# Delta rule gate stage in channel order: 512-column gate products, outputs turned on their own, gating in PSUM

## What is computed

```python
def gated_rmsnorm(o, w, gate):
    o = o * lax.rsqrt(jnp.mean(o * o, -1, keepdims=True) + RMS_EPS)
    return o * w.astype(jnp.float32) * jax.nn.silu(gate.astype(jnp.float32))

def gdn_mixer(x, w_in, conv_w, a_log, dt_bias, norm_w, w_out):
    p = x @ w_in
    qkv = causal_conv_silu(p[..., :GDN_QKV], conv_w)
    rest = p[..., GDN_QKV:]
    gate = rest[..., :GDN_VAL].reshape(B, T, GDN_HEADS, GDN_DV)
    ...
    o = gated_delta_rule(q, k, v, g, beta)
    o = gated_rmsnorm(o, norm_w, gate)
    return o.reshape(B, T, GDN_VAL).astype(x.dtype) @ w_out

x = layer_norm(DEEP_ALPHA * x + y, ln_g[i], ln_b[i])   # y: the mixer's result
```

## Time and profile before

| | |
|---|---|
| median of three runs | 1319.94 us (1319.39 to 1321.54) |
| the profiled execution | 1322.95 us |
| its span, first to last instruction | 1321.2 us |
| TensorE busy | 1232.3 us, 93% of the span |
| DVE, ScalarE, POOL busy | 600.3, 504.2, 382.8 us |
| granted TensorE clock, mean of the span | 0.967 |

### The profile page before, as it was taken

One profiled execution on the slowest core, in us unless ns is written; L12 is line 12 of the kernel. 1 busy time (PEld: TensorE's weight loads), 2 busy tenths in 40 slices (PEclk: granted clock), 3 DMA queues, 4 the chain that ended last, 5 costly groups with the idle time before them and its releaser, 6 DMA issues.

```text
span 1321.2 us, 17053 instructions
## 1 busy us (share of the span) xinstructions
PE 1232.3 (93%) x6956; PEld 1050.5 (80%) x6956; DVE 600.3 (45%) x869; ACT 504.2 (38%) x621; POOL 382.8 (29%) x92
## 2 busy tenths in 40 slices
PE   5879999999999979999999999888899799999986
PEld 5568878888788858888798878888788568999875
DVE  1473353343622255569724466444500614443614
ACT  4255434444211136643434235122221533335423
POOL 0014443444344423233212110222234225233111
PEclk9889999999999989999999999998999899999988
DMA  9983222222322332232312120111232322221101
GB/s 352 386 293 112 95 84 75 95 95 95 114 96 96 96 132 65 64 96 64 102 59 64 33 96 1 37 61 63 68 124 96 100 66 96 64 65 65 64 0 64
DMA packets 108349, 128.66 MB, mean 97 GB/s; under 512 B 13033, under 2 KB 98925, under 8 KB 108157
## 3 DMA queue, kind: packets, MB, share of 16 engines
q1 hardware_dynamic: 103412, 120.69, 27.5%
q10 hardware_dynamic: 4873, 7.04, 1.5%
HBM read 122.48 MB, written 5.24 MB: 97 GB/s over the span
## 4 chain that ended last, share of the span: by engine, by line
PE 41%; DVE 8%; ACT 2%; issue 1%; DVEq 0%; ACTq 0%
PE ps L243 10%; PE ps L244 9%; PE ps L245 9%; DVE val L1345 4%; PE ps L1480 3%; PE ps L2062 2%; PE ps L1823 1%; PE ps L1831 1%; PE ps L1860 1%; PE ps L1951 1%; PE ps L1957 1%; PE ps L1952 1%; DVE gate_silu L1341 1%; ACT gate_silu L735 1%; PE ps L2081 1%
## 5 line engine op out<-in xcount | busy, mean ns | idle before, releaser
L365 POOL TENSOR_TENSOR wl<-raw,wh 128x2048 fp32r<-128x2048 f32 x81 | 378.6, 4674 | 910.1 <-ACT wh L390 910.1
L390 ACT ACTIVATE wh<-raw 128x2048 fp32r<-128x2048 f32 x81 | 154.9, 1912 | 389.2 <-PE ps L245 389.2
L243 PE MATMUL ps<-xth,wh 128*128 128x512 f32 x672 | 270.2, 402 | 4.4 <-DVE xtl L960 3.7
L245 PE MATMUL ps<-xth,wl 128*128 128x512 f32 x672 | 263.7, 392 | 0.0
L244 PE MATMUL ps<-xtl,wh 128*128 128x512 f32 x672 | 263.5, 392 | 0.0
L243 PE MATMUL ps<-wh,xth 128*128 128x256 f32 (+1 forms) x576 | 176.0, 306 | 3.4 <-DVE xtl L853 3.4
L244 PE MATMUL ps<-wl,xth 128*128 128x256 f32 (+1 forms) x576 | 174.0, 302 | 0.0
L245 PE MATMUL ps<-wh,xtl 128*128 128x256 f32 (+1 forms) x576 | 173.4, 301 | 0.0
L243 PEld LDWEIGHTS ps<-xth,wh 128*128 128x128 f32 x672 | 127.4, 190 | 31.0 <-issue 6.5
L245 PEld LDWEIGHTS ps<-xth,wl 128*128 128x128 f32 x672 | 127.2, 189 | 27.6
L244 PEld LDWEIGHTS ps<-xtl,wh 128*128 128x128 f32 x672 | 127.5, 190 | 24.4
(11 more groups left out here) (287 smaller groups left out, 1766.7 us busy)
## 6 DMA issues: line engine op xcount, KB each, us to landing
ada<-in_ada_w SPq DMA_DIRECT2D x24, 1024.0 KB, 10.8
raw<-in_gdn_w_in SPq DMA_DIRECT2D x24, 1024.0 KB, 5.1
raw<-in_ffn_w_up SPq DMA_DIRECT2D x22, 1024.0 KB, 5.0
raw<-in_gla_w_in SPq DMA_DIRECT2D x12, 1024.0 KB, 5.0
raw<-in_ffn_w_down SPq DMA_DIRECT2D x11, 1024.0 KB, 4.8
raw<-in_gdn_w_out SPq DMA_DIRECT2D x8, 1024.0 KB, 4.8
raw<-in_gla_w_out SPq DMA_DIRECT2D x4, 1024.0 KB, 4.9
xres<-in_x SPq DMA_DIRECT2D x4, 512.0 KB, 5.8
```

The costliest lines, as they stand in the source:

```text
L243: nc.tensor.matmul(o, lh, rh, start=first, stop=False)
L245: return nc.tensor.matmul(o, ll, rh, start=False, stop=last)
L365: nc.gpsimd.tensor_tensor(wl[:, s, :], raw[:, s, :], wh[:, s, :].bitcast(f32), ALU.subtract)\
L390: nc.scalar.activation(wh[:, s, :], raw[:, s, :], ACT.Copy).then_inc(hi_done, 1)
```

## The change

- The gate is made with `col_chunk`: two pieces p = 2h and 2h + 1 of 128 channels per unit, 48 products of 512 columns, each piece in one of the banks 0 to 3.
- ScalarE scales the outputs of a head by `coef` in token order (`output_scale`, four operations), and TensorE turns them without the gate (`turn_outputs(h)`), in the middle of the second piece of the same head's unit.
- The gate times the norm weight times the turned outputs is one DVE operation per piece, in place in PSUM banks 4 to 7. The norm weight is a column there, one number per partition: it comes in with the rows at the start (`bgk_norm`, one more DMA in ScalarE's queue), and the row `norm_w` goes.
- Silu, high part and low part are made per piece; `ogt_h` and `ogt_l` are laid out by channel.
- In unit 0 of the output projection the token tiles come in the order 0, 2, 1, 3, with a wait ahead of each of the last three.

```diff
...
-    bgk_col = at("bgk_col", CONST + 5888, [LH])
+    bgk_norm = at("bgk_norm", CONST + 5888, [LH + DV // P])
...
-    gate_silu = at("gate_silu", PH + 96 * KB, [2, TT, DV])
+    gate_silu = at("gate_silu", PH + 96 * KB, [4, T])
...
-    ogt_h = at("ogt_h", PH + 32 * KB, [TT, 2 * H, P], f32r)
-    ogt_l = at("ogt_l", PH + 64 * KB, [TT, 2 * H, P], f32r)
+    ogt_h = at("ogt_h", PH + 32 * KB, [2 * H, T], f32r)
+    ogt_l = at("ogt_l", PH + 64 * KB, [2 * H, T], f32r)
...
+            act.dma_start(rows[12:14, 0, :], a["gdn_norm_w_2"][0].rearrange("(k n) -> k n", n=P)).then_inc(S("rows_in"), 16)
...
-            row(norm_w[:], a["gdn_norm_w_2"][0], "alog_in")
...
-            def gated_high(h):
-                act.wait_ge(S("og_turned"), h + 1)
-                nc.scalar.activation(ogt_h[:, :, 2 * h:2 * h + 2, :].rearrange("p t k n -> p k t n"),
-                                     bank2(4 + 2 * (h % 2)).rearrange("p (k t n) -> p k t n", k=2, n=P), ACT.Copy).then_inc(S("ogt_hi"), 1)
+            def output_scale(h):
+                act.wait_ge(S("coef_done"), 1)
+                for tt in range(TT):
+                    sc = nc.scalar.activation(val[:, tt, h, :], val[:, tt, h, :], ACT.Copy, scale=coef[:, 3, tt, h:h + 1])
+                sc.then_inc(S("o_scaled"), 1)
+            def gate_activation(p):
+                if p % 2 == 0:
+                    act.wait_ge(S("gate_half"), p // 2 + 1)
+                else:
+                    act.wait_ge(w_used, U_GIN + GIN_QK + GIN_V + p // 2 + 1)
+                if p >= 4:
+                    act.wait_ge(S("og_done"), p - 3)
+                nc.scalar.activation(gate_silu[:, p % 4, :], ps[:, p % 4, :], ACT.Silu).then_inc(S("gate_done"), 1)
+            def gated_high(p):
+                act.wait_ge(S("og_done"), p + 1)
+                nc.scalar.activation(ogt_h[:, p, :], ps[:, 4 + p % 4, :], ACT.Copy).then_inc(S("ogt_hi"), 1)
+            output_scale(0)
+            output_scale(1)
             for h in range(H):
-                act.wait_ge(w_used, U_GIN + GIN_QK + GIN_V + h + 1)
-                if h >= 2:
-                    act.wait_ge(S("og_done"), h - 1)
-                nc.scalar.activation(gate_silu[:, h % 2], bank2(2 * (h % 2)).rearrange("p (t n) -> p t n", n=DV), ACT.Silu)\
-                    .then_inc(S("gate_done"), 1)
+                gate_activation(2 * h)
+                gated_high(2 * h)
+                gate_activation(2 * h + 1)
+                gated_high(2 * h + 1)
                 high_gin(GIN_QK + GIN_V + h + 2)
-                if h >= 1:
-                    gated_high(h - 1)
-            gated_high(H - 1)
-            act.wait_ge(S("og_done"), H)
+                if h + 2 < H:
+                    output_scale(h + 2)
...
-            step(V.tensor_tensor(coef[:, 3], coef[:, 2], scal[:, QS], ALU.mult))
-            def gated_low(h):
-                v.wait_ge(S("ogt_hi"), h + 1)
-                dst = ogt_l[:, :, 2 * h:2 * h + 2, :].rearrange("p t k n -> p k t n")
-                hi = ogt_h[:, :, 2 * h:2 * h + 2, :].rearrange("p t k n -> p k t n")
-                V.tensor_tensor(dst, bank2(4 + 2 * (h % 2)).rearrange("p (k t n) -> p k t n", k=2, n=P), hi.bitcast(f32), ALU.subtract)\
-                    .then_inc(S("ogt_lo"), 1)
-            for h in range(H):
-                v.wait_ge(S("gate_done"), h + 1)
-                g = gate_silu[:, h % 2]
-                V.tensor_tensor(g, g, norm_w[:].unsqueeze(1).broadcast_to([P, TT, DV]), ALU.mult).then_inc(S("gate_scaled"), 1)
-                v.wait_ge(S("gate_scaled"), h + 1)
-                v.wait_ge(S("o_joined"), (TT - 1) * H)
-                for tt in range(TT):
-                    og = V.scalar_tensor_tensor(val[:, tt, h, :], val[:, tt, h, :], coef[:, 3, tt, h:h + 1], g[:, tt, :], ALU.mult, ALU.mult)
-                og.then_inc(S("og_done"), 1)
-                if h >= 1:
-                    gated_low(h - 1)
-            gated_low(H - 1)
+            V.tensor_tensor(coef[:, 3], coef[:, 2], scal[:, QS], ALU.mult).then_inc(S("coef_done"), 1)
+            for p in range(2 * H):
+                v.wait_ge(S("og_turned"), p // 2 + 1)
+                v.wait_ge(S("gate_done"), p + 1)
+                o = ps[:, 4 + p % 4, :]
+                V.scalar_tensor_tensor(o, o, bgk_norm[:, LH + p % 2:LH + p % 2 + 1], gate_silu[:, p % 4, :], ALU.mult, ALU.mult)\
+                    .then_inc(S("og_done"), 1)
+                v.wait_ge(S("ogt_hi"), p + 1)
+                V.tensor_tensor(ogt_l[:, p, :], o, ogt_h[:, p, :].bitcast(f32), ALU.subtract).then_inc(S("ogt_lo"), 1)
...
-                        for tts in ((0, 1), (2,), (3,)):
-                            if tts == (2,):
-                                between()
-                                pe.wait_ge(S("ogt_lo"), H - 1)
-                            if tts == (3,):
-                                pe.wait_ge(S("ogt_lo"), H)
+                        for tt in (0, 2, 1, 3):
+                            if tt in between:
+                                between[tt]()
                             for kk in range(2):
                                 ready(kk)
-                                for tt in tts:
-                                    for half in range(2):
-                                        mm = product(tt, half, kk)
+                                for half in range(2):
+                                    mm = product(tt, half, kk)
...
-            def turn_gated(h):
-                pe.wait_ge(S("og_done"), h + 1)
+            def turn_outputs(h):
+                pe.wait_ge(S("o_scaled"), h + 1)
                 if h >= 2:
-                    pe.wait_ge(S("ogt_lo"), h - 1)
+                    pe.wait_ge(S("ogt_lo"), 2 * h - 2)
                 for k in range(2):
                     for tt in range(TT):
                         mm = turn(ps[:, 4 + 2 * (h % 2) + k, tok(tt)], val[:, tt, h, k * P:(k + 1) * P])
                 mm.then_inc(S("og_turned"), 1)
-            u0 = U_GIN + GIN_QK + GIN_V
             pe.wait_ge(S("vn_done"), (TT - 1) * H)
             for h in range(H):
-                pe.wait_ge(unit_split, u0 + h + 1)
-                if h >= 2:
-                    pe.wait_ge(S("gate_done"), h - 1)
-                token_unit((u0 + h) % 2, 2 * (h % 2), (lambda: turn_gated(h - 1)) if h >= 1 else None)
-            pe.wait_ge(S("gate_done"), H)
-            down_unit(1, U_GOUT, GOUT, lambda k, tt: ogt_h[:, tt, k, :], lambda k, tt: ogt_l[:, tt, k, :],
-                      lambda k: pe.wait_ge(S("ogt_lo"), k // 2 + 1) if k % 2 == 0 or k == 2 * GOUT - 1 else None, None,
-                      lambda: turn_gated(H - 1))
+                u = U_GIN + GIN_QK + GIN_V + h
+                pe.wait_ge(unit_split, u + 1)
+                for sub in range(2):
+                    p = 2 * h + sub
+                    if p >= 4:
+                        pe.wait_ge(S("gate_done"), p - 3)
+                    between = (lambda k: turn_outputs(h) if k == KD // 2 else None) if sub == 1 else None
+                    col_chunk(u % 2, sub, ps[:, p % 4, :], between).then_inc(w_used if sub else S("gate_half"), 1)
+            pe.wait_ge(S("gate_done"), 2 * H - 2)
+            banks_free = {2: lambda: pe.wait_ge(S("ogt_lo"), 2 * H - 2), 1: lambda: pe.wait_ge(S("gate_done"), 2 * H),
+                          3: lambda: pe.wait_ge(S("ogt_lo"), 2 * H)}
+            down_unit(1, U_GOUT, GOUT, lambda k, tt: ogt_h[:, k, tok(tt)], lambda k, tt: ogt_l[:, k, tok(tt)],
+                      lambda k: pe.wait_ge(S("ogt_lo"), k + 1) if k < 2 or k == 2 * GOUT - 1 else None, None, banks_free)
```

More of the change, by code:

```diff
@@ L157, in build @@
     mask_add = at("mask_add", TMP + 12 * KB, [P])
-    norm_w = at("norm_w", TMP + 12 * KB + 512, [DV])
     junk_o = at("junk_o", TMP + 13 * KB + 512, [DV])
     coef = at("coef", CONST + 4608, [4, TT, H])
-    ogt_h = at("ogt_h", PH + 32 * KB, [TT, 2 * H, P], f32r)
-    ogt_l = at("ogt_l", PH + 64 * KB, [TT, 2 * H, P], f32r)
+    ogt_h = at("ogt_h", PH + 32 * KB, [2 * H, T], f32r)
+    ogt_l = at("ogt_l", PH + 64 * KB, [2 * H, T], f32r)
     ln_gb = at("ln_gb", PH + 96 * KB, [2, D])
@@ L444, in _ @@
             ada_cols = a["ada_b"][0].rearrange("(k n) -> k n", n=P)
[L445 to L448, removed]
+            act.dma_start(rows[12:14, 0, :], a["gdn_norm_w_2"][0].rearrange("(k n) -> k n", n=P)).then_inc(S("rows_in"), 16)
+            act.dma_start(rows[14:30, 0, :], ada_cols[0:2 * KD, :]).then_inc(S("rows_in"), 16)
+            act.dma_start(rows[30:46, 0, :], ada_cols[3 * KD:5 * KD, :]).then_inc(S("rows_in"), 16)
+            act.dma_start(rows[46:54, 0, :], a["mix_pre_g"][0].rearrange("(k n) -> k n", n=P)).then_inc(S("rows_in"), 16)
+            act.dma_start(rows[54:62, 0, :], a["ffn_pre_g"][0].rearrange("(k n) -> k n", n=P)).then_inc(S("rows_in"), 16)
             cw = a["ffn_conv_w"][0].rearrange("j (k n) -> (j k) n", n=P)
@@ L619, in _ @@
```

(14 more changed lines are left out.)

## The result

| | before | changed |
|---|---|---|
| median | 1320.74 us (4 runs, 1319.39 to 1322.07) | 1284.26 us (4 runs, 1282.71 to 1284.86) |
| span of the profiled execution | 1321.2 us | 1282.0 us |
| DVE, ScalarE busy | 600.3, 504.2 us | 551.5, 520.3 us |
| granted TensorE clock, mean | 0.967 | 0.972 |

The ratio is 0.9722, 95% interval 0.9709 to 0.9736: 36.5 us less. The forecast was 36.9 us less, 1283.0, with a range of 1280 to 1293. The base has moved a little: the forecast started from the median of three runs of the kernel before, 1319.94 us, and the fourth makes it 1320.74.

A forecast was written before the change was run, and what follows sets the result against it. Bound: TensorE waiting in the gate stage for a chain ending 2.6 us late. Terms 5.2 + 20.1 + 10 + 1.1 = 36.4, bottom up 37.4, taken as 36.9 off 1319.94: 1283.0 us, range 1280 to 1293.

The forecast's parts named there:

- What bounds: Gate stage: the 8.3 us chain to the turns ends 2.6 us late, one DVE product stretched to 4.79 us beside POOL.
- Products: Gate units: 48 products of 512 columns instead of 96 of 256, by the trace's starts 5.2 us less over eight units.
- Turns: Gate units: the eight turns per head stay in number and cost 0.93 us, no change.
- Waits and clock: Gate stage: TensorE's eight waits for DVE go, 20.1 us less, and the half clock with them, 10 us less.
- Boundary: Gate stage to output projection: the first product's wait for the silu goes, 1.1 us less.
- The sum: Gate stage and output projection: 36.4 us less by terms, 37.4 bottom up; 37.0 taken, 0.1 given back for the head.
- The new chain: Behind a gate unit's end: silu, gating, high part and weight split take 9.0 us, needed at 11.8, leaving 2.8 us.
- Head: Kernel start: one more DMA in ScalarE's queue moves the first turn by up to 0.4 us; 0.1 us taken.
- Rival A: Gate stage: turns lower the clock without a wait, once per head, 13.6 us back, 1296.6 us; chance 6%.
- Rival B: Gate stage: POOL holds DVE operations on PSUM too, split chain 1.5 us late per unit, 1295 to 1309 us; chance 7%.
- Rival C: Gate products: the wider products bring only 0.9 instead of 5.2 us, 1287.3 us; chance 4%.
- D: Gate stage: lower clock for long stretches, 512-column products 0.43 us apart, slower overall at 1368 us; chance 2%.

The follow-up runs named there:

- two runs that undo nothing but an order: The kernel before with only the next weights' split moved behind the high part (1294.29 us), or only the turns moved later in the next unit (1293.78 us).
- narrow products: The changed kernel with each gate piece made of 48 products of 256 columns in place of 24 of 512: 1288.69 us.
- late turns: The kernel before with a head's turns three quarters through the next unit instead of half: 1293.78 us.
- short waits: The changed kernel with a unit's turns also waiting for POOL's split of the next unit's weights, seven waits of 0.56 us: 1288.26 us.
- early turns: The changed kernel with the turns at the head of the second piece instead of its middle: 1284.65 us.

## Why the prediction was right, by its steps

- *What bounds.* Right, and shown by two runs that undo nothing but an order: the chain ended 2.6 us late, and what made it so long was the one held product. Either end of the chain alone gave 27 of the 36.5 us.
- *Products,* -5.2 us. By the narrow products it is 4.7 in the stage, 4.0 to 4.6 by the ratios. By the run with late turns, whose units are those of the kernel before, it is 5.1: a unit takes 12.42 us there and 11.79 in the changed kernel. (The rival's price is 0.96 us by its own formula, not 0.9.)
- *Turns,* no change: 0.87 instead of 0.93 us.
- *Waits and clock,* -30.1 us: without the last wait of 1.5 us, which the late turns leave in, that is 28.6, and 29.0 went with the late turns alone.
- *Boundary,* -1.1 us: no distance larger than 0.23 us is left there, and more than 1.1 us went. From the gate's last product to the projection's last it is 91.4 us with late turns (917.87 to 1009.23) and 87.0 in the changed kernel: 4.3 us less. Of these 0.9 is the last block of turns, which now stands in the gate stage, 1.5 and 1.1 are waits, and 0.8 is the slower restart behind them.
- *The sum.* By terms it was 36.4, bottom up 37.4, and I took 37.0 without asking what the 1.0 between them was. The stage lost 37.5. What the terms lack is above all the restart: a wait costs more than its idle time, 0.74 us for one of 0.56 in the run with short waits. The saving of the medians, 36.5 us, lies nearer to the terms, but it holds other stages too; that it met the forecast of 36.9 within 0.4 us is in part luck. The changed median, 1284.26, lies just outside the forecast's own ends of 1281.5 to 1284.
- *The new chain.* The split was expected 9.0 us behind a unit's end and stands at 8.8 (849.46, with the next unit's first product at 840.68). The silu takes 0.60 us, not 0.69; four scalings 1.7 us, where 2.8 was the bound. The slack, expected at 2.8 us, is 3.0 (the products that need these weights start at 852.46).
- *Head.* The first turn started at 11.04 instead of 11.02 us. The DMA more cost nothing.
- *Rival A,* the clock falling at turns without a wait, fell: 1.00 through 94.5 us with eight blocks of them. The Trainium skill's page "TensorE: Matmul & The Clock Gate" (section "Part 4: PE-mode transpose") has it that transposes don't count as busy; blocks of 0.87 us among products are too short to show it either way. What the rival has as its mechanism does occur in this kernel, elsewhere. In the profile of the kernel before the clock fell at 192 us without any wait, behind 4.1 us of turns and other sparse products (modulation, L1515 and L1519):

```profile
188.06 1.02 PE L1515 MATMUL ps<-ada_part,group_rows 128*128 128x512 f32 x2
...
191.12 1.13 PE L1519 MATMUL ps<-ada_rows,ident 24*128 24x256 f32 x4
192.18 0.67 PE L243 MATMUL ps<-xth,wh 128*128 128x512 f32 x1
192.65 0.63 PE L244 MATMUL ps<-xtl,wh 128*128 128x512 f32 x1
193.07 0.63 PE L245 MATMUL ps<-xth,wl 128*128 128x512 f32 x1
```

- *Rival B* fell by the early turns: the DVE operations with a PSUM operand are not held. *Rival C* fell by the narrow products. *D* did not come.

The profile showed what the forecast named, but for one place: the projection's last product was expected near 1002 us and started at 998.24, since all ahead of the gate was 3.5 us earlier. The forecast had not reckoned with that, nor with a profiled pair that differs by 39.2 us where the medians differ by 36.5.

## What to carry to other kernels

A DVE operation whose duration is ten times its neighbours' can be a wait that the list of waits does not show: look for what POOL does beside it, and either give it an operand in PSUM or move one of the two. Where TensorE waits for a chain of other engines, compare the chain's length with the place in its list where the result is wanted; moving either end by two lines can be worth most of a restructuring: here 27 of 36.5 us. Ahead of eight turns, a wait of 2.54 us cost 1.6 us more through the clock in four cases of seven, one of 0.56 us in none of seven.

## What the runs showed of the hardware that I had not expected

- Waits of equal length at equal places of a unit (seven of 2.54 us) brought the clock to 1.2 GHz behind four of them only, in the profiled execution.
- In the kernel before the clock was at 0.93 for 190 to 215 us while TensorE was busy for all 25 us. The other nine profiles, with the same turns and sparse products ahead of this place, have 1.00. Why it fell in one of ten is open.
- TensorE waits 3.3 us for DVE (L975) near 350 us in all ten profiles. The clock from 350 to 375 us was 0.86 in seven of them, 0.93 in two and 1.00 in one, the first of the changed kernel.
- A product with 256 columns and its own weight load starts 120 ns after the last, one with 512 columns 226 ns: doubling the columns saves 13.5 of 240 ns, and with 256 columns the weight loads alone are busy nearly all of the time (99.58 of 99.70 us).
